# Head of a fused two-block kernel: the first token quarter as one transfer, no touch transfer, warming in one run, and the large constants' transfer behind the fifth weight blob

## The reference

```python
h = h + mixer(rmsnorm(h, gain))      # projections of all tokens, two kinds of attention, gates, an output product
h = h + mlp(rmsnorm(h, gain2))       # two products with a nonlinearity between
```

## Time and profile before

| | us |
|---|---|
| median of 3 runs | 876.7 |
| lowest and highest | 876.62, 877.75 |
| profiled execution, its own time | 877.58 |
| span from its first to its last instruction | 875.8 |
| TensorE busy in the span | 867.3 |

### The profile page before, as it was taken

The page is one execution under the profiler, slowest core; times in us unless marked ns, Lnnn a source line. Parts: engine busy times, 40 slices in busy tenths (PEclk is TensorE's granted clock), DMA queues, the critical chain, the costliest instruction groups (busy, mean ns, idle before and its releaser), DMA issues.

```text
span 875.8 us, 13035 instructions
## 1 busy us (share of the span) xinstructions
PE 867.3 (99%) x4820; PEld 730.8 (83%) x4820; DVE 623.5 (71%) x987; ACT 459.2 (52%) x735; POOL 46.6 (5%) x83
## 2 busy tenths in 40 slices
PE   8999999999999999999999999999999999999997
PEld 6887888888888888889998777777888888888886
DVE  6857777665876666668865888787766876666665
ACT  6546534334644444454556776677643654444443
POOL 1000010000200000002000000132300100000000
PEclk9999999999999999999999999999999999999999
DMA  9955344553565555453682335333274365555531
GB/s 327 417 214 177 133 156 144 192 192 144 194 239 191 191 192 189 147 185 106 203 308 101 123 123 170 145 100 142 97 268 172 127 225 185 181 195 190 187 142 48
DMA packets 26830, 156.75 MB, mean 179 GB/s; under 512 B 3600, under 2 KB 5136, under 8 KB 9376
## 3 DMA queue, kind: packets, MB, share of 16 engines
q1 hardware_dynamic: 24048, 148.71, 47.5%
q10 hardware_dynamic: 2736, 7.42, 2.3%
HBM read 151.45 MB, written 1.05 MB: 174 GB/s over the span
## 4 chain that ended last, share of the span: by engine, by line
PE 98%; DMA 1%; DVE 0%; SPq 0%; DVEq 0%; ACTq 0%; issue 0%; ACT 0%
PE ps L495 19%; PE ps L497 18%; PE ps L496 18%; PE ps L647 15%; PE ps L651 8%; PE ps L660 4%; PE ps L1622 2%; PE ps L662 2%; PE ps L530 1%; PE ps L1557 1%; PE ps L1581 1%; PE ps L1576 1%; PE ps L1571 1%; DMA raw<-weights 1%; PE ps L1269 1%; PE ps L678 1%
## 5 line engine op out<-in xcount | busy, mean ns | idle before, releaser
L1722 DVE TENSOR_TENSOR wlo<-raw,whi 128x2048 fp32r<-128x2048 f32 x134 | 306.6, 2290 | 152.4 <-ACT whi L769 152.0
L769 ACT ACTIVATE whi<-raw 128x2048 fp32r<-128x2048 f32 x134 | 256.5, 1915 | 182.4 <-PE ps L497 111.2
L647 PE MATMUL ps<-x_all,whi 128*128 128x512 f32 x336 | 80.1, 390 | 0.0
L495 PE MATMUL ps<-whi,xT 128*128 128x512 f32 x192 | 76.8, 400 | 0.0
L497 PE MATMUL ps<-whi,xT 128*128 128x512 f32 x192 | 75.0, 391 | 0.0
L496 PE MATMUL ps<-wlo,xT 128*128 128x512 f32 x192 | 74.8, 390 | 0.0
L647 PEld LDWEIGHTS ps<-x_all,whi 128*128 128x128 f32 x336 | 62.3, 188 | 12.5
L647 PE MATMUL ps<-xT,whi 128*128 128x512 f32 x256 | 61.6, 391 | 0.0
L647 PEld LDWEIGHTS ps<-xT,whi 128*128 128x128 f32 x256 | 47.3, 188 | 9.3
L495 PE MATMUL ps<-whi,fT_h 128*128 128x512 f32 x128 | 50.3, 393 | 0.0
L496 PE MATMUL ps<-wlo,fT_h 128*128 128x512 f32 x128 | 49.9, 390 | 0.0
(11 more groups left out here) (339 smaller groups left out, 1695.6 us busy)
## 6 DMA issues: line engine op xcount, KB each, us to landing
raw<-weights SPq DMA_DIRECT2D x134, 1024.0 KB, 4.8
kswap<-kraw SPq DMA_DIRECT2D x52, 68.0 KB, 2.0
cst<-consts SPq DMA_DIRECT2D x1, 1371.0 KB, 13.0
raw<-weights SPq DMA_DIRECT2D x4, 256.0 KB, 5.6
raw<-weights SPq DMA_DIRECT2D x2, 512.0 KB, 6.9
gate_a<-gain_rows ACTq DMA_DIRECT2D x2, 512.0 KB, 7.8
gate_r<-gain_rows ACTq DMA_DIRECT2D x2, 512.0 KB, 5.9
gate_s<-gain_rows ACTq DMA_DIRECT2D x2, 512.0 KB, 6.8
```

The lines of the kernel that those rows point to most:

```text
L495: pe.matmul(o, lh, rh, start=first, stop=False)
L647: pe.matmul(ps[:, bank0 + j, :], vh[:, k, j * P:(j + 1) * P], x[:, :, k, :], start=k == 0, stop=False)
L769: act.activation(whi[s][:], raw[s][:], ACT.Copy).then_inc(split_hi, 1)
L1722: dve.tensor_tensor(wlo[s][:], raw[s][:], whi[s][:], ALU.subtract).then_inc(split_lo, 1)
```

## The change

Five edits. The touch transfer, its semaphore and ScalarE's wait for it are taken out. Token chunks 0 and 1 come as one transfer instead of two (`X_LOADS` has four entries in place of five, and the numbers of the later ones move down by one). On TensorE the warming products stand in one run ahead of the transposes (512, 512 and 256 columns, where 512 stood ahead of the first transposes and 512 and 384 behind them). The transposes of chunk 1 come ahead of the first product instead of behind it. The large constants and the row of sinks are issued behind the load of blob 4 instead of ahead of it; to that end the loads of blobs 4 to 7 are written out ahead of the loop.

```diff
--- before.py
+++ after.py
@@ -87,7 +87,7 @@
             ((0, 0), (0, 2), (0, 4), (0, 6), (1, 0), (1, 2), (1, 4), (1, 6)))
 XT_PLACE = (None, (2, 3, 4, 6, 2, 3, 5, 7), (0, 1, 4, 6, 0, 1, 5, 7), (2, 3, 4, 5, 6, 7, 4, 5))
 
-X_LOADS = ((0, 1), (1, 2), (2, 4), (4, 6), (6, 8))
+X_LOADS = ((0, 2), (2, 4), (4, 6), (6, 8))
 
 FIRST = ((0, 0, 1), (0, 1, 2), (0, 2, 3), (0, 3, 4), (1, 0, 2), (1, 2, 4))
 
@@ -335,7 +335,6 @@
         early_in = sem("early_in")
         const_in = sem("const_in")
         first_in = [sem(f"first_in{i}") for i in range(len(FIRST))]
-        touch_in = sem("touch_in")
         first_up = sem("first_up")
         first_hi = sem("first_hi")
         first_lo = sem("first_lo")
@@ -706,7 +705,6 @@
                     sp.wait_ge(split_lo, made)
                 sp.dma_start(raw[slot_of(n)][:], src).then_inc(raw_in[slot_of(n)], 16)
 
-            sp.dma_start(o_tok[1][:, 0:16], w[0][:, 0:16]).then_inc(touch_in, 16)
             sp.dma_start(cst[:, 0:EARLY], consts[:, 0:EARLY]).then_inc(early_in, 16)
 
             def load_tokens(i):
@@ -721,18 +719,21 @@
 
             load_first(0)
             load_first(1)
-            load_tokens(2)
+            load_tokens(1)
             load_first(2)
             load_first(3)
+            load_tokens(2)
+            load_first(4)
             load_tokens(3)
-            load_first(4)
-            load_tokens(4)
             load_first(5)
             load(2, w[2], None)
             load(3, w[3], None)
+            load(4, w[4], 1)
             sp.dma_start(cst[:, EARLY:NCONST], consts[:, EARLY:NCONST]).then_inc(const_in, 16)
             sp.dma_start(row[:], rows.partition_broadcast(P)).then_inc(const_in, 16)
-            with sp.Fori(4, N1 - 4, 4) as i:
+            for n in range(5, 8):
+                load(n, w[n], n - 3)
+            with sp.Fori(8, N1 - 4, 4) as i:
                 for j in range(4):
                     load(j, w[bass.ds(i + j, 1)].rearrange("a p c -> (a p) c"), i + (j - 3))
             load(N1 - 1, w[N1 - 1], N1 - 1 - 3)
@@ -815,8 +816,7 @@
                     act.activation(dst[:, 4 * half:4 * half + 4, t * P:(t + 1) * P], pieces_of(half, t), ACT.Copy,
                                    scale=scale).then_inc(mg_hi, 1)
 
-            for i in range(2):
-                act.dma_start(h[:, :, i * P:(i + 1) * P], x[:, :, i * P:(i + 1) * P]).then_inc(x_in[i], 16)
+            act.dma_start(h[:, :, 0:TOK], x[:, :, 0:TOK]).then_inc(x_in[0], 16)
 
             act.wait_ge(init_ok, 1)
             act.activation(lam[:], kaT[:, 0, 0:4], ACT.Copy)
@@ -858,7 +858,6 @@
                         act.activation(tok[0][:, t, :], ps[:, t, :], ACT.Copy,
                                        scale=stat[:, t, 3:4]).then_inc(taken_a, 1)
                 if n == 3:
-                    act.wait_ge(touch_in, 16)
                     act.wait_ge(blob_used, 3)
                     for t in range(NT):
                         rs = stat[:, t, 3:4]
@@ -1310,13 +1309,12 @@
 
             pe.wait_ge(init_ok, 1)
             warm = kaT[:].rearrange("p a k -> p (a k)")
-            keep_warm(1, 1, warm)
+            keep_warm(2, 1, warm)
+            keep_warm(1, 1, warm, TOK)
             pe.wait_ge(early_in, 16)
             first_turn(0)
-            keep_warm(1, 1, warm)
-            keep_warm(1, 1, warm, TOK + P)
+            first_turn(1)
             first_products(pe, "hh", 0)
-            first_turn(1)
             first_products(pe, "hl", 0)
             first_products(pe, "lh", 0)
             first_turn(2)
@@ -1979,8 +1977,8 @@
             first_low(6)
             first_low(7)
             first_part(5)
+            dve.wait_ge(x_in[2], 16)
             dve.wait_ge(x_in[3], 16)
-            dve.wait_ge(x_in[4], 16)
             square_upper(0)
             square_upper(1)
             add_shares(0)
```

## The result

| | before | changed |
|---|---|---|
| median of 22 runs | 877.24 us | 878.30 us |
| lowest and highest | 876.62, 877.91 | 877.28, 881.13 |
| profiled execution, its own time | 877.58 | 879.91 |
| span of the profiled execution | 875.8 | 878.1 |

A forecast was written before the change was run, and what follows sets the result against it. TensorE was taken to bound the kernel, holding 98% of the chain of waits. +0.17 us (first product late) - 0.08 (later hole) = +0.09, on a median of 876.7 giving 876.8 us; range 875.9 to 877.9.

The forecast's parts named there:

- The bound: TensorE: the end moves only by the first product's start (7.67 us) or by gaps or clock behind it.
- The scale: Whole kernel: +0.09 us in sum, put on the median's scale as 876.7 + 0.1 = 876.8 us.
- The touch: SP's queue: weights issued 0.46 us earlier, first quarter lands at 6.70 us; the gain is lost to VectorE's order.
- the touch might be worth something: Rival, first quarter: a first access cost falls on it, landing 8.4, product 8.9, +1.2, 877.9 us; chance 4%.
- The tokens as one transfer: ScalarE's queue: two issues become one, 256 KB landing at most at 5.0 us, not late for what follows.
- tokens late: Rival, ScalarE's queue: the one token transfer lands at 6.5 us, first product at 8.60, +0.9, 877.6 us; chance 4%.
- VectorE's order: VectorE in the head: chunk 0's low part precedes the cast, so the first product starts at 7.71 to 7.97, 0.17 late.
- The clock: Rival, TensorE between warming's end and first product: clock low, first products at half speed, +2.7, 879.4 us; chance 5%.
- The time of the rise: TensorE in the head: clock goes from 1.2 to 2.4 GHz at 5.9 us as before, or at 5.36.
- Chunk 1: TensorE's transposes ahead of the first product: a later 0.33 us hole may shrink, taken as 0.08 us gained.
- the constants: SP's queue: issued at about 13.1 us, landing about 25.5, 12.7 us ahead of their reader; nothing on the path.
- the fifth blob: SP's queue: lands some 3 us earlier and ends ScalarE's wait of 2.43 us; nothing on the path.

The follow-up runs named there:

- with the wait: Changed kernel, no touch, with SP waiting for VectorE's memset ahead of its first weight issue: 877.69 us, ratio 1.0005.
- the second version with that wait: Changed kernel, no touch, with SP's wait for the memset, VectorE's cast first and 256 warming columns behind chunk 1's transposes: 876.85 us, ratio 0.9995.

## Why the prediction was wrong, point by point

- **The bound.** "It can move the end in two ways only": held. The whole difference is the first product's start and the clock behind it.
- **The scale.** The shift was forecast at +0.1 us and measured at +1.06. The rest of the distance from 876.8 to 878.30, 0.54 us, is the base: the sum stood on a median of three runs, 876.7, where 22 runs give 877.24.
- **The touch.** The failed step. I priced what its removal does to the quarter behind it and looked at what else might fall on that quarter; I did not ask what the earlier quarter does to transfers already under way on another queue. The gain of 0.46 us in the issue was real, and the quarter landed at 6.4 us where 6.70 was forecast; but the one token transfer beside it went from between 4.5 and 4.9 us (with a touch, four traces) to between 5.4 and 6.9 us (without, five traces), so that the first product waited for the tokens' chain and stood at 8.81 us instead of 7.84. A rival said that the touch might be worth something, but by the wrong mechanism: a first access, not a delay.
- **The tokens as one transfer, "at most 5.0 us".** The step where it entered the sum. The row it came from, 3.6 us to landing, was measured with the weights held back by the very touch that goes. With the touch the one transfer does land at 4.8. The rival "tokens late" had the size: 6.5 us and +0.9; the thirteen runs with the higher mean clock stand 0.9 us above before. The 6.5 came from transfers queued behind weights on SP's queue, a ground that the prediction itself set aside, so the match is in part luck.
- **VectorE's order.** Held: from the transposes' start to the first product 2.10 us were worked out, 2.03 measured, and with the tokens in time the product stood at 7.89 in the predicted 7.71 to 7.97. The cast moved first took it off the chain.
- **The clock.** The rival was described rightly in place and kind, and its chance was far too small: 5%, where 8 of 22 runs show it. I counted the 0.78 us of idling before as evidence, though there warming matmuls stood right ahead of it. Its price, +2.7, was for a longer stretch; the upper group's middle is 2.3 above before, the late tokens among them. The time of the rise, put between 5.36 and 5.9 us, was bounded too narrowly as well: in six of the twelve traces with the new warming order the whole warming ran at the 1.2 GHz pace (4.63 or 4.64 us), in the shortest it took 4.00.
- **Chunk 1, the constants, the fifth blob.** Held, with the row of sinks landing 14 us ahead of its reader and ScalarE's wait gone at no gain.
- **The combination.** The two rivals were taken as exclusive. Late tokens lengthen the stretch without matmuls, and one makes the other likelier: with nothing behind the transposes, a mean clock of 0.997 or less is in 16 of 55 runs of the four versions without touch or wait, and in 4 of 45 of the four with one.

## What to carry to other kernels

Before taking out a small transfer or wait at the head of a queue, ask what it holds back: here, moving a large transfer earlier put its slow first packets beside a transfer that another engine had issued. Order an engine's program by what the first product needs (here the cast ahead of a low part that only a later product reads), so that one late input doesn't drag the rest. And put warming where the waiting is, between the last transposes and the first product, not only ahead of them; here that left no run with the lower mean clock, though a gain over the kernel before isn't shown. A row that bounds a price is only good if the thing removed wasn't what made it so.

## What was not expected of the hardware

The first packets of the weight stream are slow in the three traces looked at: in the changed kernel nine packets took 45% of the engines' time for 1 us (0.02 MB), with the wait ten took 76% of 0.5 us, and in the kernel before, touch and all, the engines moved 159 GB/s at a full share. And 0.24 us in the time of one issue moved the landing of another queue's 256 KB from between 5.4 and 6.9 us to 3.6 us, and in the second version with that wait to the same within 0.1 us.
